# Modulation tiles in pairs, sums of squares on VectorE, and another order of the opening, in a two-layer decoder step

## The reference

```python
mod = (jax.nn.silu(c) @ ada_w + ada_b)[:, None, :]      # c: one vector a sequence, 1 + 8 of them
shift1, scale1, gate1, shift2, scale2, gate2 = jnp.split(mod, 6, axis=-1)
h = rmsnorm(x, norm_g[0]) * (1.0 + scale1) + shift1
z = h @ w_in                                            # u, v | h, B, C | a, g | three branch gates
ya = u * (tril(W_s) @ layernorm(gelu(v)) + b)           # mixer A, chunks of 128
yb = bb * causal_dwconv3(cb * hb)                       # mixer B, keeps a history
yc = silu(layernorm(causal_dwconv31(ac * sigmoid(gc)))) # mixer C, keeps a history
merged = sum(sigmoid(zg_b) * (y_b @ w_branch[b]) for b in range(3))
x = x + gate1 * (merged @ w_out)
h2 = rmsnorm(x, norm_g[1]) * (1.0 + scale2) + shift2
x = x + gate2 * peer(h2)                                # 16384 experts, 8 heads, top 16
```

## Time and profile before

| | us |
|---|---|
| median of 3 runs | 4106.55 (4103.54 to 4110.15) |
| the profiled execution | 4103.9 |
| its span in the trace | 4102.1 |
| PE busy | 4008.8 |
| DVE busy | 2732.5 |
| ACT busy | 1584.2 |
| POOL busy | 812.4 |

### The profile page before, as it was taken

The page is one execution under the profiler, slowest core; times in us unless marked ns, Lnnn a source line. Parts: engine busy times, 40 slices in busy tenths (PEclk is TensorE's granted clock), DMA queues, the critical chain, the costliest instruction groups (busy, mean ns, idle before and its releaser), DMA issues.

```text
span 4102.1 us, 77256 instructions
## 1 busy us (share of the span) xinstructions
PE 4008.8 (98%) x29632; PEld 3893.8 (95%) x29632; DVE 2732.5 (67%) x4453; ACT 1584.2 (39%) x2673; POOL 812.4 (20%) x685
## 2 busy tenths in 40 slices
PE   6999999999999999999999999999999999999998
PEld 3899999999999999999989999899999999999998
DVE  2367638977666636777753775698776664477776
ACT  2222323333577733333332223333337775333332
POOL 1000000000122206555300000000002221356551
PEclk9999999999999999999999999999999999999999
DMA  4444332354466668999934532225445667799995
GB/s 171 140 113 134 103 117 77 118 166 136 128 190 193 192 202 315 345 352 352 336 128 114 134 109 83 78 89 170 136 137 160 187 190 208 238 352 345 352 349 185
DMA packets 418219, 781.87 MB, mean 191 GB/s; under 512 B 151184, under 2 KB 274448, under 8 KB 417344
## 3 DMA queue, kind: packets, MB, share of 16 engines
q1 hardware_dynamic: 176640, 441.70, 33.4%
q10 hardware_dynamic: 194240, 196.10, 15.2%
q0 software_dynamic: 47104, 141.00, 9.5%
HBM read 655.79 MB, written 122.88 MB: 190 GB/s over the span
## 4 chain that ended last, share of the span: by engine, by line
PE 95%; DVE 3%; ACT 1%; DMA 1%; issue 1%; DVEq 0%; SPq 0%; ACTq 0%; POOLq 0%
PE pg L1515 20%; PE pg L1518 19%; PE pg L1516 19%; PE pm L1827 5%; PE pg L1829 4%; PE pg L1828 4%; PE pm L1829 4%; PE pm L1828 4%; PE pg L1827 4%; PE pm L1567 3%; PE pm L1779 2%; DVE ys L1179 1%; PE pm L1542 1%; PE pm L1743 1%; DMA merged<-stream 1%; PE pm L1551 1%
## 5 line engine op out<-in xcount | busy, mean ns | idle before, releaser
L1515 PE MATMUL pg<-a_hi,w_hi 128*128 128x260 f32 x6400 | 1684.6, 284 | 25.1 <-DVE a_lo L1025 14.4
L1516 PE MATMUL pg<-a_lo,w_hi 128*128 128x260 f32 x6400 | 1667.2, 282 | 0.0
L993 DVE TENSOR_TENSOR w_lo<-raw,w_hi 128x1024 fp32r<-128x1024 f32 x688 | 841.2, 1225 | 1003.8 <-ACT w_hi L886 703.0
L1518 PE MATMUL pg<-a_hi,w_lo 128*128 128x260 f32 x6400 | 1290.0, 283 | 0.5 <-issue 0.5
L1515 PEld LDWEIGHTS pg<-a_hi,w_hi 128*128 128x128 f32 x6400 | 1208.7, 189 | 41.1 <-issue 37.1
L1516 PEld LDWEIGHTS pg<-a_lo,w_hi 128*128 128x128 f32 x6400 | 1205.6, 188 | 0.3
L1518 PEld LDWEIGHTS pg<-a_hi,w_lo 128*128 128x128 f32 x6400 | 987.1, 189 | 0.3 <-issue 0.2
L886 ACT CAST w_hi<-raw 128x1024 fp32r<-128x1024 f32 x500 | 525.7, 1051 | 784.9 <-PE pg L1829 739.6
L570 POOL DMA_INDIRECT rows<-stream,at_v x256 | 282.1, 1102 | 766.0 <-DVE acc_tok L1442 317.7
L580 POOL TENSOR_TENSOR one_j<-one_j,g_lo 128x896 fp32r<-128x896 f32 x112 | 189.3, 1690 | 1034.9 <-ACTq L914 1034.9
L618 ACT ACTIVATE hid<-pg 128x260 f32<-128x260 f32 x512 | 170.7, 386 | 517.0 <-PE pg L1518 497.1
(11 more groups left out here) (234 smaller groups left out, 5598.3 us busy)
## 6 DMA issues: line engine op xcount, KB each, us to landing
raw<-stream SPq DMA_DIRECT2D x688, 512.0 KB, 4.1
hidden_dram<-hid SPq DMA_DIRECT2D x256, 196.0 KB, 3.5
gate_dram<-gate_buf ACTq DMA_DIRECT2D x28, 1792.0 KB, 11.0
hid_in<-hidden_dram ACTq DMA_DIRECT2D x64, 784.0 KB, 6.1
gate_in<-gate_dram ACTq DMA_DIRECT2D x64, 784.0 KB, 11.0
ada_raw<-stream ACTq DMA_DIRECT2D x76, 512.0 KB, 3.4
hid_tok<-hid SPq DMA_DIRECT2D x256, 64.0 KB, 3.6
rows<-stream,at_v POOLq DMA_INDIRECT x256, 7.3
```

The costliest lines, as they stand in the source:

```text
L993: tt(ring(False, s), raw[:, s], ring(True, s).bitcast(F32), ALU.subtract).then_inc(lo_ready, 1)
L1515: pe.matmul(outs[h], w[0], a[h][0], start=first, stop=False)
L1516: pe.matmul(outs[h], w[0], a[h][1], start=False, stop=False)
L1518: mm = pe.matmul(outs[h], w[1], a[h][0], start=False, stop=last)
```

## The change

1. Modulation tiles go in pairs at every second step: 8 pairs in layer 0 for its own layer (steps 3, 5, 7, 9, 11, 13, 25, 27), 6 for the next (53 to 63), and 6 in layer 1 (7 to 27). ACT and DVE split both tiles into fp32r parts (`early_hi`, `early_lo`, or `late_hi`, `late_lo`), the condition is split likewise into `c_parts` [128, 8, 18], and `ada_pair` multiplies hi and lo part of both tiles, 256 columns each, with all 18 columns. The turn multiplies with `both_parts`, which adds the two halves of the 18 rows. Single stay 16 tiles of steps 28 to 43 in each layer, the four in the gap of layer 1, and T_O, T_O + 1 and the two in the gap behind T_O.
2. Squares are summed on DVE (`add_square`) ahead of PE: all 8 in the opening, 7 and 1 in the output projection, groups of 1, 1, 1, 2, 2, 1 between the layers and at the end. The squares have buffers of their own (`square_of`), so ACT no longer waits for PE's sums.
3. Opening: x is loaded behind the first batch; the order of batches is 2, 3, 0, 1 (scale first); batch b + 1 is begun before batch b is turned; the turn of the last comes inside the values; the sum of squares follows batch 1. Norm, casts and subtractions are interleaved by hand.
4. POOL's loads of params and histories wait for the fourth weight tile, ACT's first tile loads stand behind the four casts. The loads for the pair of step 5 are issued among the casts of step T_V.
5. Between the layers the cast of the fourth tile comes behind the squares.

```diff
@@ the plan of the tiles
-OWN_STEPS = (3, 3, 4, 5, *range(6, 14), *range(T_BB, T_BR), *range(T_BR, T_BR + 16))
+FIRST_ORDER = (2, 3, 0, 1)
+PAIR_EARLY, PAIR_LATE = (3, 5, 7, 9, 11, 13, T_BB + 1, T_BB + 3), tuple(range(T_BR + 25, T_O, 2))
+OWN_STEPS = (*(w for w in PAIR_EARLY for _ in range(2)), *range(T_BR, T_BR + 16))
-NEXT_STEPS = (*range(T_BR + 24, T_O + 2), GAP_2, GAP_2)
+NEXT_STEPS = (*(w for w in PAIR_LATE for _ in range(2)), T_O, T_O + 1, GAP_2, GAP_2)
+def sq_groups(j):
+    if j == 0:
+        return [[*range(KC)]]
+    return [[*range(KC - 1)], [KC - 1]] if j % 2 else [[0], [1], [2], [3, 4], [5, 6], [7]]
@@ SP, opening
-            for b in range(FIRST_BATCHES):
-                sp.dma_start(first_tiles[b], stream[4 * b:4 * b + 4].rearrange("n p k m -> p n k m")).then_inc(first_in[b], 16)
+            for b, n in enumerate(FIRST_ORDER):
+                sp.dma_start(first_tiles[b], stream[4 * n:4 * n + 4].rearrange("n p k m -> p n k m")).then_inc(first_in[b], 16)
                 if b == 0:
+                    sp.dma_start(x[:, :, :], x_t).then_inc(x_in, 16)
                     sp.dma_start(ada_par[:, :, :], ada_params).then_inc(ada_par_in, 16)
-                if b == 1:
-                    sp.dma_start(x[:, :, :], x_t).then_inc(x_in, 16)
@@ POOL, ahead of params and histories
+                else:
+                    pool.wait_ge(raw_in[3], 16)
@@ ACT
+            def pair_hi(l, w):
...
+                act.wait_ge(ada_used, g)
...
+                for z in range(2):
+                    n = RAW_TILES.index(g + z)
+                    act.wait_ge(ada_in[n % 2], (n // 2 + 1) * 16)
+                    act.copy(pair_parts(w)[0][:, z], ada_raw[:, n % 2]).then_inc(pair_hi_ready, 1)
@@ ACT, opening
+                    act.wait_ge(x_in, 16)
+                    for n in range(KC):
+                        square(l, 0, n)
+                    ada_rows(0)
+                    ada_rows(1)
+                    std(l, 0, 1.0 / D)
+                    for k in range(4):
+                        split(l, 0, k)
                     for g in loads_first(0):
                         load_ada(g)
...
                     ada_rows(2)
@@ ACT, between the layers
+                    act.wait_ge(prod, (l - 1) * NM + (M_ED + NBLK))
+                    split(l, 0, 3)
+                    std(l, 0, 1.0 / D)
@@ ACT, behind read_product of step n (and so at T_U, T_BB, T_BR)
+                    pair_hi(l, n + 1)
                     split(l, 1, 8 + 2 * c)
@@ DVE
+            def add_square(l, base, n):
...
+                own.link(tt(sum_, sum_, square_of(l * 2 + base, n), ALU.add))
+            def pair_lo(l, w):
...
+                for z in range(2):
+                    dve.wait_ge(pair_hi_ready, 2 * pairs_before(g) + z + 1)
+                    tt(lo[:, z], ada_raw[:, RAW_TILES.index(g + z) % 2], hi[:, z].bitcast(F32), ALU.subtract).then_inc(pair_lo_ready, 1)
@@ DVE, norm of the opening
+                    for k in range(4):
+                        scaled(k)
+                        if k:
+                            split(l, k - 1, k - 1)
+                    take_ada(2)
+                    scaled(4)
+                    low(0, 1)
+                    split(l, 3, 3)
@@ DVE, behind the last update of x
+                for n in (4, 6):
+                    add_square(l + 1, 0, n)
@@ PE
             def first_ada(b):
...
                 for k in range(KC):
+                    if b >= 1 and k == KC // 2:
+                        ada_turn(b - 1)
+            def ada_pair(g):
...
+                pe.wait_ge(pair_lo_ready, 2 * pairs_before(g) + 2)
+                out = ada_bank(b)[0:2 * NC, 2 * h * P:2 * (h + 1) * P].rearrange("p (s m) -> p s m", s=2)
+                for k in range(KC):
+                    for z, part in enumerate(pair_parts(TILE_STEP[g][1])):
+                        mm = pe.matmul(out, c_parts[:, k, :], part[:, :, k, :], start=k + z == 0, stop=k + z == KC)
+                mm.then_inc(ada_used, 2)
@@ PE, output projection
                     ada_step(l, T_O + k)
-                    if k >= 2:
-                        square_sum(l, 1, k - 2)
-                square_sum(l, 1, KC - 2)
+                square_sum(l, 1, 0)
                 gap = tiles_at(l, GAP_2)
                 for g in gap[0:1]:
                     ada_tile(g)
-                square_sum(l, 1, KC - 1)
+                square_sum(l, 1, 1)
```

More of the change, by code:

```diff
@@ L91, in tiles_at, with paired, pair_at, pairs_before @@
     return [g for g in TILE_STEP if TILE_STEP[g] == (l, w)]
+def paired(g):
+    return TILE_STEP.get(g, (0, 0))[1] in PAIR_EARLY + PAIR_LATE
+def pair_at(l, w):
+    return next((g for g in tiles_at(l, w) if paired(g)), None)
+def pairs_before(g):
+    return sum(paired(i) for i in TILE_STEP if i < g) // 2
 def before(g):
@@ L122, with sq_sums_by, sq_adds_by @@
 G_END = G_FROM + NSUB
+def sq_groups(j):
+    if j == 0:
+        return [[*range(KC)]]
+    return [[*range(KC - 1)], [KC - 1]] if j % 2 else [[0], [1], [2], [3, 4], [5, 6], [7]]
+def sq_sums_by(j, g):
+    return sum(len(sq_groups(i)) for i in range(j)) + g + 1
+def sq_adds_by(j, g):
+    return sum(len(s) > 1 for i in range(j) for s in sq_groups(i)) + sum(len(s) > 1 for s in sq_groups(j)[0:g + 1])
 def row_turns(l, k):
@@ L515, in _ @@
             own.settle()
+            own.link(pool.tensor_tensor(both_parts[:, :], ident[0:2 * NC, 0:NC], ident[0:2 * NC, NC:2 * NC], ALU.add))
             pool.sem_inc(consts, 1)
@@ L645, in ada_rows @@
                 act.wait_ge(ada_used, 4 * (b + 1))
-                own.link(act.copy(ada_row[:, :], ada_bank(b)[0:NC, :]))
+                if 0 < b < FIRST_BATCHES:
+                    act.wait_ge(ada_prod, b)
+                rows = 2 * NC if paired(4 * b) else NC
+                own.link(act.copy(ada_row[0:rows, :], ada_bank(b)[0:rows, :]))
                 act.sem_inc(ada_row_ready, 1)
@@ L730, in _ @@
                     act.sem_inc(v_gelu, 1)
+                freed = loads_at(l, T_U)
                 for k in range(4):
                     split(l, 1, k)
+                    if freed and k % 2:
+                        act.wait_ge(ada_used, before(freed[k // 2]) + 1)
+                        load_ada(freed[k // 2])
                 act.wait_ge(v_stats, l + 1)
@@ L961, in _ @@
                         own.restart()
-                for block in range(NBLK - 4 if l == DEPTH - 1 else NBLK):
+                for block in range(NBLK - 4 if l == DEPTH - 1 else NBLK - 1):
                     act.wait_ge(prod, l * NM + (M_ED + block + 1))
@@ new lines, in shifted_samples, with low_samples @@
+                def shifted_samples():
+                    own.link(tt(of_samples, of_samples, mod[:, at:at + KC, 1:NC], ALU.add))
+                    dve.sem_inc(nb_ready, 1)
+                def low_samples(n):
+                    dve.wait_ge(hi_of_nb, nth + n)
+                    own.link(tt(samples(a_lo), of_samples, samples(a_hi).bitcast(F32), ALU.subtract))
+                if l == 0 and w == 0:
+                    for k in range(4):
+                        scaled(k)
[5 more added lines that the diff above has]
+                    split(l, 3, 3)
+                    for k in range(1, 4):
+                        low(k, k + 1)
+                        scaled(k + 4)
+                    scaled_samples()
+                    take_ada(3)
+                    shifted_samples()
+                    low(4, 5)
+                    low(5, 6)
+                    low_samples(7)
+                    low(6, 8)
+                    low(7, 9)
+                    return
@@ L1066, in _ @@
                 if l == 0:
-                    for b in range(FIRST_BATCHES - 1):
-                        take_ada(b)
-                    split(l, 0, 0)
-                    split(l, 1, 1)
-                    take_ada(FIRST_BATCHES - 1)
+                    for n in range(1, KC):
+                        add_square(l, 0, n)
+                    take_ada(0)
+                    root(0)
+                    take_ada(1)
                     scale_of(l, 0)
-                    dve.wait_ge(x_in, 16)
-                split(l, 2, 2)
-                split(l, 3, 3)
+                else:
+                    split(l, 2, 2)
+                    split(l, 3, 3)
+                    root(l * 2)
                 norm(l, 0)
                 ada_taken(l, GAP_1 + 2)
+                if l == 0:
+                    pair_lo(l, T_V + 3)
                 own.restart()
@@ L1289, in _ @@
                 scale_of(l, 1)
+                root(l * 2 + 1)
                 norm(l, 1)
@@ L1599, in _ @@
                     pe.wait_ge(x_smp, l)
-                    for n in range(KC):
-                        square_sum(l, 0, n)
+                    for g in range(len(sq_groups(l * 2))):
+                        square_sum(l, 0, g)
                     ada_step(l, GAP_1)
@@ L1852, in _ @@
             pe.wait_ge(x_smp, DEPTH)
-            for n in range(KC):
-                square_sum(DEPTH, 0, n)
```

(2 more changed lines are left out.)

159 lines of the change are left out of this document (111 added, 48 removed).

## The result

The changed kernel takes 4052.9 us in the median of four runs (4049.05 to 4064.06), the kernel before, on the same chip, 4106.2; the ratio is 0.9874 (0.9852 to 0.9896). It is faster by 53.3 us. I had predicted 4024.0 and a gain of 82.8, so some 29 us of the gain are missing, and the time lies above my range. The profiled execution took 4050.53 us, its span 4048.8.

What follows compares the result with a forecast made beforehand. TensorE, busy for 98% of the span, was taken as the bound. Gains of 36.0 + 30.6 + 8.9 + 5.3 + 2.0 = 82.8 us off 4103.9 gave 4021.1, as a median 4023.8, taken as 4024.0; range 4013 to 4040.

Steps and rivals of the forecast that it cites:

- The opening: Start to product 6 of layer 0: values start at 44.0 against 70.52, product 6 at 89.7 against 125.70; gain 36.0 us.
- The pairs' own price: Modulation pairs in both layers: 2.1 us each against 3.9 for two tiles, saving 1.8; 18 save 32.4 us.
- The sums in the output projection of layer 0: Five sums of squares leave from between products, 4.0 us, and a sixth before the last tile, 0.9.
- between the layers: Sums of squares between the layers: six for eight, and a later tile cast, move the end by 5.3 us.
- The wait that I had put at step 63 of layer 0: End of T_BR: 0.83 us at step 63's product, first output products another 1.0 later; 1.8 us taken off.
- First failed step: Loads of pairs: issued 11.7 us ahead of need, so a load may take 8.2 us; median landing 3.4 us.
- rival E: Pairs' loads land late, PE waits, slower than before; whole gain gone at a landing of 10.7 us; chance 0.02.
- Second failed step: T_BB: DVE falls about 2 us behind with two pairs, which the double buffer covers and the next steps clear.
- D: ACT and DVE fall behind: 0.5 to 1.0 us of wait at each of 20 pairs, 4034 to 4044; chance 0.12.
- B: Opening gives less: PE idles between batches 0 and 1, values start at 51 to 54, 4031 to 4034; chance 0.12.
- C: Pair matmuls run at two records each, so a pair takes 3.6 us: 4054; chance 0.05.
- F: More gain than forecast, 4008 to 4015, if DVE and the buffers cover the late steps; chance 0.03.

Runs made afterwards that it cites:

- experiment 9: Changed kernel with pair buffers freed on the lo part, later history stores and plain turns: 4020.8 us, again 4022.1; with turns kept as products: 4026.5 us.
- turns_apart: Changed kernel with paired turns as plain transposes whose halves VectorE adds: 4049.1 us, 0.9857 of the kernel before.
- Experiment 3: Also spelled load28_ahead: changed kernel with the loads for steps 28 and 29 issued ahead of ScalarE's wait for src_ready: 4035.6 us, 0.9826 of the kernel before.
- free_on_lo: Changed kernel with a pair's buffer, from step 25 on, loaded anew once VectorE has made the lo part: 4051.0 us, 0.9821 of the kernel before.
- stores_later: Changed kernel with GpSimd's five history stores started some 60 us later: 4043.7 us, 0.9845 of the kernel before.
- load28_ahead: The same run as Experiment 3: 4035.6 us.

## Why the prediction was right and wrong

**What held.** The opening, 36.2 us for 36.0; the first batch came at 10.36 instead of 9.4 and the second at 20.61 instead of 19.8, and the batches behind took as much less than I had put down. The rate that I had taken from the row held: 421 GB/s from 20 to 28 us. (Two of my additions there are off by 0.1 to 0.2 us: they give 28.5 and 66.8.) The pairs' own price: matmuls start 0.12 us apart, a pair takes 1.86 (I had 2.1) and saves 1.8 over all. The sums in the output projection of layer 0, 4.6 for 4.9; between the layers, 5.5 for 5.3. The clock stayed at 1.00 behind the start of the values. The wait that I had put at step 63 of layer 0 came one product later, 0.86 us before the first output product; a longer one, 1.73 us at product 56, I had not named. With the two late loads and the turns mended the kernel takes 4020.8, 3 us below the number I had given; with the turns kept, 4026.5.

**First failed step: the landing of a pair's loads.** "so a load may take 8.2 us; there 512 KB took 3.4 us in the median", and of rival E, "Only landings in the crowded first 20 us were so long". The median was over 43 loads; the question was about the two that are issued in T_BB, beside the history stores, and the trace of before had the two loads of T_BB at 11.8 us. By rival E's own price (a landing of 8.9 and 10.6 against 8.2, and 1.6 us for the slowed work) the loss at step 27 would have come out at 2.4 + 1.6 = 4.0 us; it was 3.6 and 4.4. The mechanism was written down, and I gave it to all pairs or none; it happened at one pair in each layer. Cost: 8.0 us.

**Second failed step: the tile behind the last pair was not looked at.** "It falls about 2 us behind, which the double buffer covers and the next steps clear." The double buffer is what the pair takes away. The pair of step 27 holds both buffers, so the load of step 28 has to go out afterwards, and on ACT there stood a wait in front of it that the kernel before had too and that was harmless there. I had listed what the pairs add to ACT and DVE, but not where the next single tile's issue comes in ACT's order. Cost: 8.0 + 7.8 = 15.8 us.

**Third: the turns.** A product of a whole fp32 matrix needs two records where a transpose needs one; the eight records of 18 rows are 0.98 us for 0.34. The edit is in the change, and the sum has no term for it, so it stood at nothing without a reason. Cost: 6.4 us by these rows, ten turns; the kernels of experiment 9 differ by 5.4 us in the timelines up to the keys and by 4.4 us in the totals.

**Sizes.** From product 52 to the first output product the kernel before takes 94.1 us and the changed one 85.9. With 1.3 us for the two paired turns in it, the six late pairs gave 9.4 us, and I had 10.8 less 1.8. The two waits there, 1.73 and 0.86 us, were more than the 1.8 that I took off, and the pair being 0.2 us cheaper than I had it made up for it. 23.8 + 6.4 = 30.2 against 29.5 missing: the remainder is within what the runs can tell. That the rest fits so closely is in part luck. In layer 1 PE waits 3.19 us before product 4, and behind it the product took 5.85 us in this trace, as the clock stayed at 1.00; in that of turns_apart the same wait was followed by 0.50, and the product took 8.6.

**The rivals.** D spoke of DVE in T_BB, "over-full for two pairs". DVE was indeed late there, but as a link: its taps held src_ready, src_ready held ACT, and ACT held the load. Experiment 3 took it out of the chain without giving DVE any less to do. E's mechanism, the late landing, is the first failed step. B, C and F did not happen.

## What to carry to other kernels

When a change takes both halves of a double buffer at once, look at the first user behind it: where its load is issued, and every wait that stands in front of that issue on the issuing engine. Take the landing of a transfer from the loads of the very stretch, not from a median over five hundred microseconds; here the stores of small pieces were what to look for. And price a wait of PE by what comes behind it as well: for the four waits of the changed kernel in T_BB this was 0.4 to 0.8 of the wait again, for a wait of 3.05 us in another run it was nothing.

## What the runs showed of the hardware

**Stores in small pieces cost the DMA engines more by the byte.** The list of queues of the changed kernel, 219.5 to 235 us (packets, MB, share of 16 engines' time; q0 has GpSimd's stores, q1 SP's tiles, q10 ACT's tiles):

```profile
q0 software_dynamic: 106, 0.25, 40.5%
q1 hardware_dynamic: 279, 1.03, 38.5%
q10 hardware_dynamic: 287, 1.05, 21.7%
```

Per MB the stores take 8 times as much of the engines' time as ACT's tiles (1.62 against 0.207) and 4 times as much as SP's (0.374), and the loads of the pair beside them land after 8.9 and 10.6 us, in free_on_lo after 12.4 and 14.4, where stores_later has 3.7 in the median. The Trainium skill, DMA: Bandwidth & Descriptors, section "Why small descriptors are slow (HBM only)", gives a fixed overhead for each packet and 27% for pieces of 256 bytes. The trace agrees in direction and is far above that size; which part of it is the pieces, and which the direction or the issuing engine, no run here separates.

**The clock.** At step 27 waits of 1.26, 1.31 and 1.67 us were followed by a granted clock of 1.00; those of 1.91, 2.04, 2.14, 2.81, 2.84, 2.86 and 3.58 us by 0.50, that is 1.2 instead of 2.4 GHz, for the pair and a part of the product, 1.3 to 1.6 us more in each case. That waits as short as these would do it I had not expected. But the length of a wait does not settle it: 3.05 us at the same place, in load28_ahead, was followed by 1.00. Nor is it the place: a wait of 3.18 or 3.19 us before product 4 of layer 1 stands in all fourteen traces. In four of them, the changed kernel among these, the product behind it took 5.85 us; in the other ten it took 7.2 to 8.6. The windows of PE behind this wait, in the changed kernel and in turns_apart:

```profile
2087.00:2091.00 4.00, 3.89 (x32) 1.00 0.59 175
...
2083.00:2087.00 4.00, 3.48 (x16) 0.50 0.54 180
```

That is a difference of 2.8 us in one product, in a place that the edit of turns_apart does not touch, and one more reason not to read much into small differences between totals. What decides it no run here shows.
